# A hybrid trunk on Trainium2: ring units over low and high parts of a tile, first pair picked in turned form, last gated product first

## The chip, the cores and the metric

The kernel runs on one core of a Trainium2 chip. Its engines are TensorE (PE, with its weight loads shown as PEld), VectorE (DVE), ScalarE (ACT), GpSimd (POOL) and SyncE (SP), which here only issues DMAs. The metric is the device time of one execution in microseconds; of several runs the median counts.

## What is computed

One layer of a decoder trunk over 512 tokens of width 1024, everything in float32: RMSNorm, four token mixers with gates, an output projection, and a mixture of experts. The change touches what comes from the output projection on:

```python
x = x + h @ w_out                          # (512, 1024), h: gated sum of the mixers
xn = rms_norm(x, ffn_norm_g)
# router: the best of 4 groups, then the best 2 of its 8 experts, with weights
for e in range(32):                        # 32 experts, hidden width 256
    hid = silu(t @ w_expert_gate[e]) * (t @ w_expert_up[e])
    out = out + combine[:, e:e + 1] * (hid @ w_expert_down[e])
return rms_norm(x + out, final_norm_g)
```

Every expert has three matrices of 1 MB: 96 MB of weights for the experts alone.

## The kernel before

Tokens are handled in four tiles of 128 (NT = 4); width 1024 is KC = 8 chunks of 128. All engines run programs of their own, written out by hand, and meet at semaphores only.

**Output products** (from L1990 on, products at L1999). Eight groups n = 0 to 7: the first four make columns 0 to 511 of the four tiles, the second four columns 512 to 1023. Each is 8 chunks of three products (high and low parts of h and w_out: hh, hl, woh, wol). Between the chunks stand the router's transposes (L1948), its logits (L1958) and the rank counts (rank_products, L1969) of the tile before. DVE adds the residual (L1108) and picks experts (`route`), ACT squares.

**First pair.** Experts run in pairs, with up to 64 tokens of each. For the first pair DVE makes 0/1 columns `chosen`, and TensorE picks the tokens' rows of x2 by products with them (choose_rows, L2005): `chosen` are the weights, x2 the moving operand of 512 columns, and the result lies in banks 0 and 1 with tokens on partitions. ACT (L1014) and DVE (L1430) copy the two banks to `xg[:, 0]`; TensorE turns them chunk by chunk (x_transposes, L2112), and DVE multiplies them with the norm's gain into xT (x_out, L1451). For all later turns GpSimd gathers rows from x2_dram by indirect DMA (L717) into xg. `first_table` makes the table of slots (L2022, L1977) after the last choose_rows.

**Expert turns** (expert_pass, L2110 to L2190 for TensorE). 17 turns: 15 whole pairs, and two further ones for the fullest expert and its partner. A turn is gate products and up products (L2146), hid = up times silu(gate) on DVE (L1087, a helper's line), two transposes (L2155), and down products (L2172). Results of a turn are scattered to y_dram by GpSimd (L724); those of the last two turns (KEPT) stay on chip as yeh and yel and are added by products with `pick` (kept_products, L2077).

**Ring of weights.** SP loads 1 MB units (load_unit_no, L518), in the order gate, gate, up, up, down, down of every pair, into NU = 21 slots (raw_slots), unit w into slot w mod 21. A unit above 20 waits until the products that read its slot are done (wait_reuse). The first 21 are loaded as room comes free: 10 before the output products, units 10 to 13 after their first half, 14 and 15 (ring_p0 over hl of tiles 0 and 1, ring_p1 over hh of tiles 0 and 1) after tile 1 of the second half, 16 to 20 (ring_e0, ring_e1 over parts of woh and wol, ring_q over hh of tiles 2 and 3) after all output products. In the same queue stand the stores of x2 (L567), one for each tile.

**End.** SP waits for the scatters, loads the gathered results y of tile 1 (EARLY_ROWS), the last two down units, then the results of tiles 0, 2, 3 and the final gain gfin, spread over all partitions. DVE adds weighted results (gather_results), in turn LAST for tile 1 before it makes hid. TensorE sums in PSUM (TOTALS) for tiles 0 and 1; DVE adds PSUM sums for tiles 2 and 3 (added, L1658). ACT squares with a sum, and takes the root (final_norm, L1059, L1061); DVE scales with the reciprocal and gfin (scaled, L1650, L1087), in the order 0, 2, 1, 3, and SP stores (L608). The code after `If(most > SLOT)` handles experts with more tokens and is not run on these inputs.

## Time and profile before

| | |
|---|---|
| three runs | 720.05, 722.11, 722.59 us; median 722.11 us |
| profiled execution | 720.5 us, its span 718.4 us |
| TensorE clock granted, mean | 0.995 of full speed |
| busy | PE 97%, PEld 72%, DVE 52%, ACT 36%, POOL 11% |
| DMA | 163.52 MB, mean 228 GB/s |
| chain that ended last | PE 90%, DMA 4%, DVE 3% |

The profile is one execution. A busy TensorE is not one at its peak, as products are pipelined. The page's slices of the span (40 equal ones, 18 us each, busy share in tenths) show when an engine works; the windows view gives the same for stretches that one names, with the share of time in which the 16 DMA engines were busy and what they moved. "[0.82 <-DVE chosen L1391]" behind an instruction says that its engine was idle for 0.82 us before it, and what ended that.

### The profile page before, as it was taken

The page shows a single profiled execution, that of the slowest core. Times are in us where ns is not written, and L with a number is a line of the kernel's source. Part 1 is how long each engine was busy: PE and PEld are TensorE (multiplying, and loading weights), DVE is VectorE, ACT ScalarE, POOL GpSimd, SP SyncE. Part 2 cuts the span into 40 slices and gives each one's busy share as a digit, 9 for nine tenths or more (in the row PEclk, how much of TensorE's full clock was granted, in tenths as well). Part 3 has the DMA queues.
Part 4 walks back from the last instruction along what each step waited for, and adds up shares of the span by engine and source line. Part 5 has one row for each costly group of instructions (what it writes and reads, how often), then busy time and mean ns, then how long its engine had stood idle before and what let it go on. Part 6 is the DMA issues. An engine that isn't in the chain of part 4 may idle for free.

```text
span 718.4 us, 10092 instructions
## 1 busy us (share of the span) xinstructions
PE 698.4 (97%) x3967; PEld 514.5 (72%) x3967; DVE 371.8 (52%) x727; ACT 256.4 (36%) x426; POOL 80.1 (11%) x116
## 2 busy tenths in 40 slices
PE   7999999999999999999999999999999999999894
PEld 6888987877877777788888888665555556555442
DVE  6378996357676778755536303751514121212227
ACT  7332134467676776644225212121101111111113
POOL 2001922000010101000003000011211212121000
PEclk9999999999999999999999999999999999999998
DMA  7523244220212222295214598699999999999993
GB/s 240 174 66 111 65 121 147 74 73 16 68 66 73 74 74 74 82 381 181 91 56 183 219 416 303 266 368 365 408 418 419 401 421 421 418 420 417 419 375 141
DMA packets 60208, 163.52 MB, mean 228 GB/s; under 512 B 7846, under 2 KB 39667, under 8 KB 47868
## 3 DMA queue, kind: packets, MB, share of 16 engines
q1 hardware_dynamic: 54668, 150.71, 55.3%
q0 software_dynamic: 5488, 12.11, 4.5%
q8 instruction: 33, 0.54, 0.3%
q14 instruction: 19, 0.16, 0.1%
HBM read 154.64 MB, written 15.99 MB: 238 GB/s over the span
## 4 chain that ended last, share of the span: by engine, by line
PE 90%; DMA 4%; DVE 3%; ACT 1%; issue 1%; SPq 0%; POOLq 0%; DVEq 0%; ACTq 0%
PE psum L1719 31%; PE psum L2146 15%; PE psum L1820 12%; PE psum L2172 8%; PE psum L1999 6%; PE psum L1832 3%; PE psum L2112 2%; DMA ring_e<-y_dram 2%; DVE ring_e L1087 2%; PE psum L1845 1%; PE psum L1875 1%; DMA y_dram<-ye,slots 1%; PE psum L2155 1%; PE psum L1958 1%; PE psum L1910 1%; PE psum L1898 1%
## 5 line engine op out<-in xcount | busy, mean ns | idle before, releaser
L1719 PE MATMUL psum<-xh,wh 128*128 128x512 f32 x256 | 99.9, 390 | 0.8 <-DVE xl L1087 0.8
L1719 PE MATMUL psum<-xh,wl 128*128 128x512 f32 x256 | 99.6, 389 | 0.0
L1719 PE MATMUL psum<-xl,wh 128*128 128x512 f32 x256 | 99.6, 389 | 0.0
L1090 DVE TENSOR_TENSOR wl<-raw,wh 128x1280 fp32r<-128x1280 f32 (+4 forms) x37 | 71.8, 1945 | 24.7 <-ACT wh L780 9.0
L1087 DVE SCALAR_TENSOR_TENSOR hid<-psum,rslot,act_g 128x256 f32<-128x256 f32 x17 | 8.2, 483 | 93.4 <-PE psum L2146 92.8
L1719 PEld LDWEIGHTS psum<-xh,wh 128*128 128x128 f32 x256 | 48.1, 188 | 11.1 <-DVE xl L1087 1.0
L1719 PEld LDWEIGHTS psum<-xh,wl 128*128 128x128 f32 x256 | 48.0, 188 | 9.9
L1719 PEld LDWEIGHTS psum<-xl,wh 128*128 128x128 f32 x256 | 48.1, 188 | 9.8
L1820 PE MATMUL psum<-xh,wh 128*128 128x512 f32 x128 | 51.7, 404 | 0.0
L1820 PE MATMUL psum<-xh,wl 128*128 128x512 f32 x128 | 50.1, 391 | 0.0
L1820 PE MATMUL psum<-xl,wh 128*128 128x512 f32 x128 | 49.9, 390 | 0.0
L1087 DVE SCALAR_TENSOR_TENSOR sg<-cu,ch,sg 128x512 f32<-128x512 f32 x60 | 48.7, 882 | 0.0
L2146 PE MATMUL psum<-ring_w,xT 128*64 128x256 f32 x256 | 38.8, 383 | 0.0
L1036 ACT ACTIVATE act_g<-psum,rslot 128x256 f32<-128x256 f32 x17 | 8.1, 474 | 78.5 <-PE psum L2146 72.7
L1038 ACT ACTIVATE hidT<-psum 128x256 f32<-128x256 f32 x17 | 6.5, 384 | 78.1 <-PE psum L2155 78.1
L1640 DVE COPY ye<-psum 128x512 f32<-128x512 f32 x15 | 10.4, 691 | 44.6 <-PE psum L2172 44.6
L724 POOL DMA_INDIRECT y_dram<-ye,slots x15 | 15.1, 1009 | 158.0 <-DVE ye L1640 114.5
L1311 DVE TENSOR_TENSOR gp<-gs,psum 128x512 f32<-128x512 f32 x16 | 11.0, 687 | 36.9 <-PE psum L1719 36.1
L2146 PEld LDWEIGHTS psum<-ring_w,xT 128*64 128x64 f32 x256 | 22.3, 136 | 10.5 <-issue 3.4
L958 ACT ACTIVATE gs<-psum,bg 128x512 f32<-128x512 f32 x16 | 10.9, 687 | 50.3 <-PE psum L1719 50.3
L1820 PEld LDWEIGHTS psum<-xh,wl 128*128 128x128 f32 x128 | 24.0, 188 | 5.2
L1820 PEld LDWEIGHTS psum<-xl,wh 128*128 128x128 f32 x128 | 24.1, 188 | 4.8 <-issue 0.2
(386 smaller groups left out, 1539.6 us busy)
## 6 DMA issues: line engine op xcount, KB each, us to landing
raw<-in_w_gate SPq DMA_DIRECT2D x16, 1024.0 KB, 6.4
raw<-in_w_in SPq DMA_DIRECT2D x9, 1024.0 KB, 5.5
ring_w<-in_w_expert_gate SPq DMA_DIRECT2D x8, 1024.0 KB, 19.8
ring_w<-in_w_expert_up SPq DMA_DIRECT2D x8, 1024.0 KB, 22.4
ring_h<-in_w_expert_down SPq DMA_DIRECT2D x8, 1024.0 KB, 16.5
ring_h<-in_w_expert_gate SPq DMA_DIRECT2D x6, 1024.0 KB, 18.2
ring_e<-in_w_expert_down SPq DMA_DIRECT2D x6, 1024.0 KB, 23.1
ring_e<-in_w_expert_gate SPq DMA_DIRECT2D x6, 1024.0 KB, 21.4
```

Source lines behind the costliest of these rows:

```text
L724: pool.indirect_dma_start(out=y_dram[:, :], out_offset=bass.IndirectOffsetOnAxis(ap=slots[n, p], axis=0), in_=ye[n, :], in_offset=None, bo ...
L958: act.activation(gs[:, m, :], gate_bank(cg, m)[:, :], ACT.Sigmoid, bias=bg[:, d:d + 1]).then_inc(S["gate_mul"], 1)
L1087: return dve.scalar_tensor_tensor(out=out_, in0=a, scalar=s, in1=b, op0=o0, op1=o1)
L1090: return dve.tensor_tensor(dst, src, hi.bitcast(F32), ALU.subtract)
L1311: dve.tensor_tensor(gp[:, m, :], gs[:, m, :], branch_bank(cg, m)[:, :], ALU.mult).then_inc(S["gate_free"], 1)
L1719: last = nc.tensor.matmul(dst, a, b, start=start and n == 0, stop=stop and n == len(seq) - 1)
L1820: last = nc.tensor.matmul(bank[6 + n % 2][:, :], a[:, c, f], b[:, c, :], start=c == 0 and q == 0, stop=c == KC - 1 and q == 2)
L1832: last = nc.tensor.matmul(bank[4 + n % 2][:, :], a[:, j, f], b[g][:, j, :], start=j == 0 and q == 0, stop=j == BJ - 1 and q == 2)
L1999: last = nc.tensor.matmul(bank[t][:, :], x_[:, t, c, :], w_[:, b, c, :], start=c == 0 and m == 0, stop=c == KC - 1 and m == 2)
L2112: last = nc.tensor.transpose(bank[b][:, (k % 4) * P:(k % 4 + 1) * P], xg[:, s, :].rearrange("p (n c) -> p c n", c=KC)[:, k, :], ident[:, :])
L2146: last = nc.tensor.matmul(dst[half, 0:FE], xT[:, k, half], w[h][:, k, :], start=k == 0, stop=k == KC - 1)
L2172: last = nc.tensor.matmul(bank[5 + b][half, :], hidT[:, m, half], w_d[h][:, m, b * T:(b + 1) * T], start=m == 0, stop=m == FE // P - 1)
```

## The change

1. **Ring slots over the parts of one tile.** ring_p0, ring_p1, xg and ring_q become one buffer ring_p of shape [2, NT, D]: [0, t] lies over hl of tile t, [1, t] over hh of tile t. Slots 14, 15 and 16 are its tiles 0, 1 and 2, each of two runs of 1024 values per partition; xg (and yel) is tile 3. Slots 17 to 20 are ring_e0 and ring_e1, first their first units, which lie over chunks 0 to 3 of woh and wol. All slots, and the source of all loads, are written as [2, 1024] per partition.
2. **Release.** Unit 14 + t is loaded after output tile t of the second half, ahead of the tile's store of x2; 17 and 18 after chunk 3 of the last tile (out_ps is raised there too), 19 and 20 after its end.
3. **First pair.** choose_rows takes the chunks of x2 as weights and `chosen` as moving operand, 8 products of 128 columns for a tile, so that the result lies turned in banks 0 and 1. The copies to xg and the first x_transposes go. GpSimd clears both halves of xg rather than one.
4. **Last gated product first.** In turn LAST gather_results for tile 1 follows hid.
5. **Tile 0's norm.** DVE takes the reciprocal of tile 0 only; ACT scales tile 0 (ACT.Copy with a scale), GpSimd multiplies with gfin, SP stores it first.

The rest of the diff counts semaphores anew.

```diff
-        ring_p0 = sb(moe, "ring_p0", [1, UNIT_E])
         kept_l = region()
-        yel = sb(kept_l, "yel", [KEPT, D], F32R)
+        yel = sb(kept_l, "yel", [KEPT, NT, D], F32R)[:, :, NT - 1, :]
         kept_l.close()
-        xg = sb(moe, "xg", [2, D])
-        ring_p1 = sb(moe, "ring_p1", [1, UNIT_E])
-        ring_q = sb(moe, "ring_q", [1, UNIT_E])
+        ring_p = sb(moe, "ring_p", [2, NT, D])
+        xg = ring_p[:, :, NT - 1, :]
...
-        raw_slots = ([r[:, n, :] for r in (ring_z, ring_x) for n in range(2)] + [ring_y[:, n, :] for n in range(2)]
-                     + [ring_w[:, n, :] for n in range(4)] + [ring_h0[:, 0, :], ring_h0[:, 1, :], ring_h1[:, 0, :], ring_h2[:, 0, :]]
-                     + [ring_p0[:, 0, :], ring_p1[:, 0, :]] + [r[:, n, :] for r in (ring_e0, ring_e1) for n in range(2)]
-                     + [ring_q[:, 0, :]])
-        AFTER_GATES, AFTER_HALF, AFTER_PAIR, AFTER_OUT = 10, 14, 16, 21
+        raw_slots = [r[:, n, :].rearrange("p (j n) -> p j n", j=2) for r, n in (
+            [(r, n) for r in (ring_z, ring_x, ring_y) for n in range(2)] + [(ring_w, n) for n in range(4)]
+            + [(ring_h0, 0), (ring_h0, 1), (ring_h1, 0), (ring_h2, 0)])]
+        raw_slots += [ring_p[:, :, t, :] for t in range(NT - 1)]
+        raw_slots += [r[:, n, :].rearrange("p (j n) -> p j n", j=2) for n in range(2) for r in (ring_e0, ring_e1)]
+        AFTER_GATES, AFTER_HALF, AFTER_TILES, AFTER_PART, AFTER_OUT = 10, 14, 17, 19, 21
...
-        yt = [raw_slots[n].rearrange("p (j n) -> p j n", j=2) for n in (16, 17, 18, 19)]
-        gfin = raw_slots[20][:, 0:D]
+        yt = raw_slots[16:20]
+        gfin = raw_slots[20][:, 0, :]
...
-                sp_e.dma_start(raw_slots[slot], weights(*units_of(c)[w], found)).then_inc(ring_full[slot], 16)
+                sp_e.dma_start(raw_slots[slot], weights(*units_of(c)[w], found).rearrange("p (j n) -> p j n", j=2)).then_inc(ring_full[slot], 16)
...
             for t in range(NT):
+                if t == NT - 1:
+                    sp_e.wait_ge(S["out_ps"], 2 * NT)
+                    for w in range(AFTER_TILES, AFTER_PART):
+                        load_unit_no(w)
+                else:
+                    sp_e.wait_ge(S["out_ps"], NT + t + 1)
+                    load_unit_no(AFTER_HALF + t)
                 sp_e.wait_ge(S["x2_ready"], NT + t + 1)
                 sp_e.dma_start(x2_dram[t * P:(t + 1) * P, :], x2[:, t, :]).then_inc(S["x2_out"], 16)
-                if t == 1:
-                    sp_e.wait_ge(S["out_ps"], NT + 2)
-                    for w in range(AFTER_HALF, AFTER_PAIR):
-                        load_unit_no(w)
-            sp_e.wait_ge(S["out_ps"], 2 * NT)
-            for w in range(AFTER_PAIR, AFTER_OUT):
+            sp_e.wait_ge(S["out_ps"], 2 * NT + 1)
+            for w in range(AFTER_PART, AFTER_OUT):
...
+                    if base == 0 and t == 0:
+                        continue
+                    sp_e.wait_ge(S["fin_last"], base + n + (1 if base else 0))
                     sp_e.dma_start(out_v[t], yt[t][:, 1, :]).then_inc(S["out_done"], 16)
...
+            sp_e.wait_ge(S["norm_step"], 3)
+            sp_e.dma_start(out_v[0], yt[0][:, 1, :]).then_inc(S["out_done"], 16)
             store_results(0)
...
-            pool.wait_ge(S["out_ps"], 2 * NT)
-            st.link(pool.memset(xg[:, 1, :], 0.0))
+            pool.wait_ge(S["out_ps"], 2 * NT + 1)
+            st.link(pool.memset(xg[:, :, :], 0.0))
...
+            pool.wait_ge(S["tab_in"], 48)
+            pool.wait_ge(S["norm_step"], 2)
+            pool.tensor_tensor(halves(yt[0][:, 1, :]), halves(yt[0][:, 1, :]), halves(gfin), ALU.mult).then_inc(S["norm_step"], 1)
...
-            act.wait_ge(S["routed_ps"], NT + 1)
-            act.activation(xg[:, 0, 0:T], bank[0][:, :], ACT.Copy).then_inc(S["moved_a"], 1)
...
                 if t < ADDED:
                     act.wait_ge(S["c_ps"], SUMMED.index(t) + 1)
                     final_norm(n, t, TOTALS[t], 3 * NT)
+                    if t == 0:
+                        act.wait_ge(S["comb"], 3)
+                        act.activation(halves(yt[0][:, 1, :]), TOTALS[0], ACT.Copy, scale=stat[:, 2, 0:1]).then_inc(S["norm_step"], 1)
...
-                dve.wait_ge(S["out_ps"], b * NT + t + 1)
+                dve.wait_ge(S["out_ps"], 2 * NT + 1 if b and t == NT - 1 else b * NT + t + 1)
...
-            dve.wait_ge(S["routed_ps"], NT + 2)
-            dve.tensor_copy(xg[:, 0, T:2 * T], bank[1][:, :]).then_inc(S["hot_ready"], 1)
...
-                        gather_results(1, EARLY_ROWS)
                     dve.wait_ge(S["silu"], E + 1)
                     dve.wait_ge(S["gu_done"], E + 1)
                     stt(hid[:, :], bank[3][:, 0:FE], rslot[:, column(c, i)], act_g[:, :], ALU.mult, ALU.mult).then_inc(S["hid_r"], 1)
+                    if isinstance(c, int) and i == LAST:
+                        gather_results(1, EARLY_ROWS)
...
+            dve.wait_ge(S["root"], NT + 2 + NORMED.index(0))
+            dve.reciprocal(stat[:, 2, 0:1], stat[:, 1, 0:1]).then_inc(S["comb"], 1)
             added(2)
-            first_scaled(0)
             added(3)
             first_scaled(2)
             first_scaled(1)
             first_scaled(3)
...
+                    if n == 2 * NT - 1 and c == KC // 2 - 1:
+                        last.then_inc(S["out_ps"], 1)
                 last.then_inc(S["out_ps"], 1)
             def choose_rows(t, b):

                 pe.wait_ge(S["hot_ready"], CHOSEN[t])
-                return nc.tensor.matmul(bank[b][:, :], chosen[:, t, :], x2[:, t, b * T:(b + 1) * T], start=t == 0, stop=t == NT - 1)
+                for k in range(4 * b, 4 * b + 4):
+                    last = nc.tensor.matmul(bank[b][:, (k % 4) * P:(k % 4 + 1) * P], x2[:, t, :].rearrange("p (n c) -> p c n", c=KC)[:, k, :],
+                                            chosen[:, t, :], start=t == 0 and k % 4 == 0, stop=t == NT - 1, skip_group_check=True)
+                return last
...
-                choose_rows(NT - 1, b).then_inc(S["routed_ps"], 1)
+                choose_rows(NT - 1, b).then_inc(S["xt_ps"], 1)
...
-                if isinstance(c, int) and i == 0:
-                    pe.wait_ge(S["moved_a"], 2 * NT + 1)
-                    pe.wait_ge(S["hot_ready"], ALL_HITS + 1)
-                elif b == 0:
+                if b == 0:
...
-                for b in range(2):
-                    x_transposes(c, 0, first % 2, b)
+                if not isinstance(c, int):
+                    for b in range(2):
+                        x_transposes(c, 0, first % 2, b)
...
-                        w = [loaded(h, kind).rearrange("p (c f) -> p c f", f=FE) for h in halves]
+                        w = [loaded(h, kind).rearrange("p j (c f) -> p j c f", f=FE) for h in halves]
...
-                                last = nc.tensor.matmul(dst[half, 0:FE], xT[:, k, half], w[h][:, k, :], start=k == 0, stop=k == KC - 1)
+                                last = nc.tensor.matmul(dst[half, 0:FE], xT[:, k, half], w[h][:, k // 4, k % 4, :], start=k == 0, stop=k == KC - 1)
...
-                    w_d = [loaded(h, 2).rearrange("p (m n) -> p m n", m=FE // P) for h in halves]
+                    w_d = [loaded(h, 2) for h in halves]
```

## Rows read from the trace of the kernel before

**Rows 1.** The page: busy share of the DMA engines in tenths, 40 slices of the span.
```profile
DMA  7523244220212222295214598699999999999993
```
**Rows 2.** Windows: stretch, its us, busy per engine, PEclk, DMA share, GB/s.
```profile
456.00:458.00 2.00, 2.00 (x12) 1.69 (x12) 1.54 (x8) 0.00 (x0) 0.00 (x0) 1.00 0.01 4
...
474.00:476.00 2.00, 2.00 (x22) 1.60 (x20) 1.70 (x13) 1.53 (x3) 1.63 (x2) 1.00 0.86 303
...
660.00:680.00 20.00, 17.13 (x118) 10.13 (x116) 4.42 (x7) 2.19 (x5) 1.01 (x1) 1.00 1.02 420
```
**Rows 3.** DMA view: us to landing of loads issued at 462.7, 475.4, 642.1, 677.5.
```profile
ring_q<-in_w_expert_up SPq DMA_DIRECT2D x1, 1024.0 KB, 14.4
...
ring_z<-in_w_expert_up SPq DMA_DIRECT2D x1, 1024.0 KB, 7.0
...
ring_x<-in_w_expert_up SPq DMA_DIRECT2D x1, 1024.0 KB, 29.4
...
ring_h<-in_w_expert_down SPq DMA_DIRECT2D x1, 1024.0 KB, 17.5
```
**Rows 4.** Timeline of PE, turns 15 and 16: start, us, what, idle before.
```profile
671.65 3.67 PE L2146 MATMUL psum<-ring_x,xT 128*64 128x256 f32 x32 [1.34 <-DMA ring_x<-in_w_expert_up]
...
695.50 3.65 PE L2172 MATMUL psum<-ring_h,hidT 128*64 128x512 f32 x16
```
**Rows 5.** Timeline, the end: VectorE and ScalarE.
```profile
692.68 0.48 DVE L1087 SCALAR_TENSOR_TENSOR hid<-psum,rslot,act_g 128x256 f32<-128x256 f32 x1
...
700.59 1.27 DVE L1087 SCALAR_TENSOR_TENSOR ring_e<-ring_e,cw,x 128x1024 f32<-128x1024 f32 x1
...
712.62 1.28 DVE L1087 SCALAR_TENSOR_TENSOR ring_e<-ring_e,stat,ring_q 128x1024 f32<-128x1024 f32 x1
...
709.14 1.02 ACT L1059 ACTIVATE ring_e<-psum 128x1024 f32<-128x1024 f32 x1 [0.49 <-PE psum L2077]
```
**Rows 6.** Timeline of SP's issues around the output products' second half.
```profile
439.15 7.23 SPq L567 DMA_DIRECT2D x_dram<-x  x2
...
460.39 1.25 SPq L518 DMA_DIRECT2D ring_e<-in_w_expert_down  x2
...
475.40 0.33 SPq L518 DMA_DIRECT2D ring_z<-in_w_expert_up  x1
```
**Rows 7.** Timeline of PE from the choosing products to the first gate product.
```profile
462.38 3.68 PE L2005 MATMUL psum<-x,chosen 128*128 128x512 f32 x8
...
467.20 1.98 PE L2005 MATMUL psum<-x,chosen 128*128 128x512 f32 x4 [0.82 <-DVE chosen L1391]
...
470.06 1.12 PE L2112 MATMUL psum<-ident,xg 128*128 128x128 f32 x8
471.69 0.65 PE L2146 MATMUL psum<-ring_z,xT 128*64 128x256 f32 x4 [0.51 <-DVE xT L1451]
```
**Rows 8.** Timeline of VectorE in the same stretch.
```profile
465.82 0.24 DVE L1087 SCALAR_TENSOR_TENSOR rmask<-re,rs,ro 128x32 bf16<-128x32 f32 x1
...
468.42 0.48 DVE L1380 TENSOR_SCALAR hot<-slot_no,rank 128x128 fp32r<-128x128 f32 x2
```
**Rows 9.** Timeline of PEld: eight weight loads of transposes and of router logits.
```profile
470.03 0.95 PEld L2112 LDWEIGHTS psum<-ident,xg 128*128 128x128 f32 x8
...
461.46 0.97 PEld L1958 LDWEIGHTS psum<-wr,xt 128*128 128x128 f32 x8
```
**Rows 10.** DMA view of 691 to 695, mostly packets of 4 KB.
```profile
DMA packets 386, 1.64 MB, mean 410 GB/s; under 512 B 42, under 2 KB 42, under 8 KB 330
```
**Rows 11.** Timeline: a GpSimd addition; one beside VectorE; VectorE alone.
```profile
85.47 3.42 POOL L665 TENSOR_TENSOR axb<-axb,gs 128x512 f32<-128x512 f32 x1
...
173.13 0.74 POOL L682 TENSOR_TENSOR run<-run,sp 128x256 f32<-128x256 f32 x1
...
173.29 1.00 DVE L1090 TENSOR_TENSOR spl<-sp,sph 128x384 fp32r<-128x384 f32 x1
...
178.36 0.56 DVE L1090 TENSOR_TENSOR run_l<-run,run_h 128x384 fp32r<-128x384 f32 x1 [0.63 <-ACT run_h L949]
```

More of the change, by code:

```diff
@@ L308, in hybrid_trunk @@
             "hi_part xg_ps xg_neg xg_min xg_ln xg_max xg_exp xb_ps xg_free gate_ps br_ps gate_free gate_mul h_add h_hi h_split out_ps x2_ready "
-            "wo_in wo_hi wo_split g_in tab_in x2_out xt2_ps moved_a lg_ps sq2_sum wr_ready slots_in flag_ready lg_act lg_in m_ready routed_ps "
+            "wo_in wo_hi wo_split g_in tab_in x2_out xt2_ps moved_a lg_ps norm_step wr_ready slots_in flag_ready lg_act lg_in m_ready routed_ps "
             "hot_ready slot_ps idx_ready over_ready rs_in rs_ps rs_ready rank_ready turns gf0 gf1 w_ps pick_ready y_hi y_lo y_zero xt_ps xe g_done gu_done silu hid_r "
@@ L623, in _ @@
                 load_results(range(NT))
-                store_results(NT)
+                store_results(NT - 1)
                 sp_e.wait_ge(S["out_done"], 2 * (16 * NT))
@@ L1009, in _ @@
                 token_squares(n)
-            act.wait_ge(S["sq2_sum"], 1)
+            act.wait_ge(S["norm_step"], 1)
             act.activation(stat[:, 1, :], stat[:, 0, :], ACT.Sqrt, bias=eps[:, 0:1], scale=1.0 / D).then_inc(S["root"], 1)
-            act.wait_ge(S["routed_ps"], NT + 1)
-            act.activation(xg[:, 0, 0:T], bank[0][:, :], ACT.Copy).then_inc(S["moved_a"], 1)
             act.wait_ge(S["lg_in"], 1)
@@ L1067, in _ @@
                     final_norm(n, t, TOTALS[t], 3 * NT)
+                    if t == 0:
+                        act.wait_ge(S["comb"], 3)
+                        act.activation(halves(yt[0][:, 1, :]), TOTALS[0], ACT.Copy, scale=stat[:, 2, 0:1]).then_inc(S["norm_step"], 1)
                 else:
-                    act.wait_ge(S["comb"], 2 + t - ADDED + 1)
+                    act.wait_ge(S["comb"], 3 + t - ADDED + 1)
                     final_norm(n, t, halves(yt[t][:, 0, :]), 3 * NT)
@@ L1077, in _ @@
                 for n, t in enumerate(NORMED):
-                    act.wait_ge(S["fin_last"], NT + n)
+                    act.wait_ge(S["fin_last"], NT - 1 + n)
                     final_norm(n, t, TOTALS[t], 4 * NT)
@@ L1422, in _ @@
             dve.wait_ge(S["sq_done"], 3 * NT)
-            dve.reduce_sum(stat[:, 0, :], sq_part[:, :, :], AX.X).then_inc(S["sq2_sum"], 1)
+            dve.reduce_sum(stat[:, 0, :], sq_part[:, :, :], AX.X).then_inc(S["norm_step"], 1)
             for part in range(2):
@@ L1671, in _ @@
             with dve.If(most[0] > SLOT):
-                dve.wait_ge(S["comb"], 2 + NT - ADDED)
+                dve.wait_ge(S["comb"], 3 + NT - ADDED)
                 for t in range(NT):
@@ L2064, in table_products @@
                 if i == SPILL and k == 0:
-                    pe.wait_ge(S["hot_ready"], ALL_HITS + 2)
+                    pe.wait_ge(S["hot_ready"], ALL_HITS + 1)
                     slot_products()
@@ L2188, in _ @@
                 with pe.Fori(1, PASSES) as c:
-                    pe.wait_ge(S["hot_ready"], c + (ALL_HITS + 2))
+                    pe.wait_ge(S["hot_ready"], c + (ALL_HITS + 1))
                     slot_products()
```

1 line of the change is left out of this document (removed).

## The prediction

> **What bounds the kernel now.** I read the windows view first. From 500 us on the 16 DMA engines are busy all the time [rows 1], in 660 to 680 at 420 GB/s while TensorE has 2.9 us idle [rows 2]. The landings say which of the two decides. A unit issued at 475.4 lands 7.0 us later, the second up unit of turn 15, issued at 642.1, after 29.4 us, at 671.5 [rows 3]: the queue falls further behind in every turn, and the 21 units loaded ahead pay for it until they are used up. That happens in turn 15: TensorE starts the up products at 671.65 after a wait of 1.34 us for that load [rows 4]. The last down unit was issued at 677.5 and landed 17.5 us later, at 695.0 [rows 3], and the last down products started at 695.5 [rows 4]. So the end of the expert stage is set by the DMA queue, not by TensorE. Its length is fixed; what counts is when it gets its work, and that is when ring units come free. After 700 the chain is VectorE: four gathered rows, four additions and four scalings nearly without a gap, from 700.59 to the last scaling at 712.62 [rows 5], then a store.
>
> The queue has one large hole: a share of 0.01 in 456 to 458 [rows 2], because the last five ring units are issued only when the last tile of output products ends (460.4 and after) [rows 6]. Unit 20 of them took 14.4 us from 462.7, so landed at 477.1 [rows 3], just after turn 0 released the first slots and two more loads went out at 475.4 [rows 6].
>
> **The change part by part.**
>
> *First pair picked in turned form.* Now: choose_rows for the last tile (467.20), the slot table, then eight transposes (470.06) of rows that ACT and DVE first had to copy to xg, then DVE's xT, then the gate products at 471.69 [rows 7]. After: no copies, no transposes; DVE's xT can start when DVE is free of its last hot columns, 468.42 + 0.48 = 468.9 [rows 8], so its first half is ready at 469.65 and TensorE goes from the table (ends 470.1) straight into the gate products. Gain 471.69 - 470.1 = 1.6 us, and DVE's tables and the first gathers follow as much earlier. The price is in choose_rows: one tile was 2 products of 512 columns, 4 instructions of about 0.43 us, since eight of them took 3.68 with the end of the last [rows 7]: 1.7 us. It becomes 8 products of 128 columns, 16 instructions, each with its own weights. The trace shows no such product. Nearest are eight transposes of 128 columns, whose weight loads follow each other at (0.95 - 0.19) / 7 = 0.109 us, and eight instructions of ordinary fp32 products with 36 columns at (0.97 - 0.19) / 7 = 0.111 [rows 9]. 16 x 0.11 = 1.8 us: the same as before. I take 0.11, the value of both rows. Tiles 1 and 2 then end at about 462.4 + 3.6 = 466.0, which just meets rmask at 465.82 + 0.24 [rows 8]; beyond 0.11 each instruction is on the path.
>
> *Ring units released tile by tile.* Units 14, 15, 16 go out as tiles 0, 1, 2 of the second half end (about 438.5, 445.5, 452.5: the store of tile 0 starts at 439.15, the loads behind the store of tile 3 at 460.39, so a tile takes about 7 us [rows 6]), 17 and 18 in the middle of the last tile (about 455.5), 19 and 20 at 460.4. In SP's queue the stores of x2 stand between them: each is still behind its own tile, and the last one, at 460.0, is now behind 5 us of loads, landing near 465; only the first gather needs it, which comes behind DVE's slot columns, after 470. The ring is then full at about 468 rather than 477. But this alone only moves the hole: there are 21 slots either way, and the 22nd load must wait for turn 0. What is gained is that the queue is empty when turn 0 releases slots, where before it still had about 1.5 us of unit 20 to do. Against that, the releases of turn 0 come more slowly than an empty queue serves them (three pairs, one behind each kind of product, the first at 475.4 [rows 6]), so part is lost again: before, the share was already down to 0.86 in 474 to 476 [rows 2]. I work with 0.7 of the 1.5, bounds 0 and 1.5.
>
> The shift of all releases by 1.6 us moves the end of the DMA queue by the full 1.6, since the work after it is the same. TensorE shifts by 1.6 too and has waits for loads in turn 15 to give up, 1.34 us in one of them alone [rows 4], so it follows the DMA.
>
> *Rows of a unit cut in two.* Slots 14, 15, 16 now consist of two runs of 4 KB per partition instead of one of 8 KB. The stretch of mostly 8 KB packets moved 420 GB/s [rows 2], one of mostly 4 KB packets 410 [rows 10]: 2.4% less, 0.06 us of the 2.5 us that 1 MB takes at 420 GB/s. Nine such units go out after turn 0 begins: 0.5 us. Sum for the DMA end: 1.6 + 0.7 - 0.5 = 1.8 us earlier (bounds 1.1 to 2.6).
>
> *Last gated product first.* DVE now adds the early gathered rows (two of 1.28) before the last hid, which therefore follows them without a gap at 692.68 [rows 5], though its up products ended near 691.6. Moved behind it, hid comes 1.0 us earlier. But the down products behind it need the last down unit, which lands at 695.0, 0.5 us before they start now [rows 3, 4]. Only 0.45 us can be had. The gathered rows themselves are needed by nothing before 700: free.
>
> *Tile 0's norm off VectorE.* One scaling of 1.28 and its reciprocal of 0.15 leave the DVE chain, 0.15 comes back: 1.28 less [rows 5]. ACT gets a copy of 1.03 us, in an idle stretch, GpSimd a product of 128 x 1024. What is late next: ACT squares tile 1 at 709.14, right behind TensorE [rows 5], so its root is there at about 710.6 (1.02 and the two small steps behind it, 0.5), DVE's scaling of tile 1 fills 710.6 to 712.05 (0.15 + 1.28), and the one of tile 3 can start at 712.2 instead of 712.62. So 0.4 us are left of the 1.28. GpSimd took 0.74 us for 256 columns, in another place 3.42 for 512 [rows 11], so 3.0 to 6.8 us for 1024. Started near 705 it ends by 708 to 712; the last store waits on SP behind it only from 711.3 on. Also DVE is slowed beside it: a difference of 384 columns took 1.00 us when GpSimd ran an addition of 0.74, and 0.56 alone [rows 11]. One scaling (two operands from SBUF) lies beside the GpSimd product; with the same ratio it costs 0.4 to 1.0 us, of which about 0.5 is free. I take 0.45 lost, bounds 0 and 1.0. So the rows show interference; the Trainium skill (GPSIMD Engine Reference, Specifications) says that GpSimd's SBUF interfaces are shared with VectorE and contend with instructions that have two SBUF inputs, which agrees with the 0.56 against 1.00.
>
> *The rest:* clearing both xg slots is 1.9 instead of 0.95 us of GpSimd at 459.3, with 12 us until the first gather; the view of weights as [2, 4, 256] has the same addresses in all slots but three; both cost nothing on the path.
>
> **Sum.** 1.8 + 0.45 + 0.4 - 0.45 = 2.2 us. The profiled execution took 720.5 us (span 718.4 and 2.1 around it) and would take 718.3. The median of the three runs is 722.1, 1.6 above the profiled one, with 2.5 us between the lowest and the highest. The same 2.2 off the median, with a little for the uncertain term of GpSimd, is 719.8.
>
> **Rivals.**
> 1. *Every unit is cut in two.* The change rewrites all loads as [2, 1024] per partition. If the transfer is not put together again where the two halves touch, all units after turn 0, some 75, cost 0.06 more: 4.5 us instead of 0.5 in a queue that sets the end. The result is 2.2 - 4.0, so 1.8 us slower: 723.9. Without any cut unit the gain is 2.7; the point from which the change loses is 2.7 / 0.06 = 45 cut units. For it: the text of the loads. Against it: the two halves are contiguous on both sides in 18 of 21 slots. Packet counts under 8 KB tell it at once. The Trainium skill (DMA: Bandwidth & Descriptors, Why a DMA increments its semaphore by 16 and not by 1) says that one descriptor moves one contiguous run of the last dimension; taken by the letter that is this rival. No row of before shows which it is. Chance 0.15.
> 2. *The turned products are slower than 0.11 us an instruction,* say 0.17, as when a weight load is not hidden behind the product before it. Then 16 take 2.7 us: 0.5 late at tile 0, 1.7 at tiles 1 and 2, 0.9 at tile 3, some of it shared with DVE's waits; the 1.6 us gain becomes a loss near 1.0. Result 2.2 - 2.6: 722.5. Against it: both nearest rows have 0.11 with a new weight load for every instruction. Chance 0.10.
> 3. *The early ring units are worth more,* the full 1.5 us, and GpSimd disturbs nothing: gain 3.5, 718.6. With a measured median on the kind side this is beyond 0.5%. Chance 0.15.
> 4. Forecast, 719.8, own range 718.5 to 721.2: chance 0.60.
>
> **Chances.** 0.5% is 3.6 us, about what a measurement of this kernel can tell from no change. Case 4 reaches that only by the spread of medians (one in six, 0.10), case 3 in about half: faster 0.18. Slower by more than 3.6 us needs rival 1 with a larger price for a cut unit (with 3% it would be 5.6 us) and an unkind median: 0.06. The rest, 0.76, is no change that can be told. Range 717.4 to 723.6: it leaves out the far ends of cases 1 and 3.
>
> **What would show it.** First gate products at 470.1 instead of 471.7, with no transposes before; 48 more instructions of choose_rows at 0.11 us; a DMA share near 1 in 446 to 452 and a new hole between 468 and 474; last down unit landing at about 693.2; last hid some 2.8 us earlier; last store at about 711.7 instead of 713.9. Packets under 8 KB up by some 3000 (12 units) if the halves are joined, by over 20000 if not. Wrong would be: an unchanged landing of the last down unit with the earlier turn 0, or a GpSimd product that ends after 711.

## The result: 8 us slower

| | before | after |
|---|---|---|
| runs | 4: 720.05 to 722.59 us, median 721.3 | 4: 727.46 to 730.62 us, median 729.74 |
| ratio | | 1.0106, 95% interval 1.0073 to 1.014 |
| profiled execution | 720.5 us, span 718.4 | 730.62 us, span 728.4 |

The prediction was 719.8, range 717.4 to 723.6: wrong in sign and outside its range. The profiled executions lie 10.0 us apart in span, so this is the difference that the rows have to explain.

The page of the kernel after: the clock granted to TensorE, the DMA share, and packets.

```profile
PEclk9999999999999999999999999979999999999998
DMA  7523234221212121493305789839999999999993
DMA packets 61745, 163.53 MB, mean 225 GB/s; under 512 B 7846, under 2 KB 39667, under 8 KB 50940
```

The DMA row has a new hole (the 3 in the 27th slice, 473 to 492 us; before a 9 [rows 1]) and PEclk has its only 7 in the same slice. The timeline of TensorE in that stretch, after (start, us, what, xcount, idle before it):

```profile
461.38 2.07 PE L2018 MATMUL psum<-chosen,x 128*128 128x128 f32 x8
...
464.25 7.86 PE L2018 MATMUL psum<-chosen,x 128*128 128x128 f32 x32
...
472.90 4.18 PE L2018 MATMUL psum<-chosen,x 128*128 128x128 f32 x16 [0.70 <-DVE chosen L1401]
...
477.03 1.87 PE L1987 MATMUL psum<-rv,hot 128*128 128x32 f32 x8
478.83 6.47 PE L2159 MATMUL psum<-ring_z,xT 128*64 128x256 f32 x32
```

L2018 is choose_rows. Its 32 instructions for tiles 1 and 2 take 7.86 us, the 16 for tile 3 take 4.18; by [rows 7] it was 3.68 and 1.98. The gate products start at 478.83, 7.1 us later than in [rows 7], and take 6.47 us. At full clock the same 32 instructions take 3.67, as in the kernels below. The weight loads of the picking set the pace:

```profile
464.23 7.70 PEld L2018 LDWEIGHTS psum<-chosen,x 128*128 128x128 f32 x32
472.90 3.89 PEld L2018 LDWEIGHTS psum<-chosen,x 128*128 128x128 f32 x16 [0.80 <-DVE chosen L1401]
```

They follow each other at 0.24 us, where the weight loads of [rows 9] had 0.11. The windows show the clock (column behind the five engines) and the DMA share:

```profile
472.00:474.00 2.00, 1.30 (x10) 1.20 (x8) 1.50 (x12) 0.00 (x0) 0.00 (x0) 1.00 0.00 0
474.00:476.00 2.00, 2.00 (x10) 2.00 (x10) 1.27 (x5) 0.00 (x0) 0.00 (x0) 0.57 0.00 0
...
480.00:482.00 2.00, 2.00 (x12) 1.08 (x10) 1.67 (x10) 1.03 (x3) 1.27 (x2) 0.50 0.00 0
```

By these windows the granted clock falls to 0.50, the 1.2 GHz level, near 474.3, and it is back near 484.5 (0.87 in 484 to 486). Before the fall lie 15 us in which TensorE had mostly these slow products and one pause of 0.70. The queue of loads is empty all that time; before, the share in 474 to 476 was 0.86 [rows 2]. Unit 21 is issued at 485.35, not at 475.40 [rows 6].

**Where the 10 us are.** From the first picking product (459.16, before 459.04) to the first up product (485.13, before 475.17) after needs 25.97 us and before 16.13: 9.84 more. With the 0.12 us of the later start, up products and unit 21 are 10.0 late. The last down unit is issued and lands so:

```profile
ring_h<-in_w_expert_down SPq DMA_DIRECT2D x1, 1024.0 KB, 18.7
```

Issued at 687.04, landed at 705.74, 10.7 later than in [rows 3]. From there to the start of the last scaling it is 16.92 us, before 17.62: the tail has gained 0.70. The queue loses another 0.7 behind unit 21, as much as the tail gains, so 10.0 + 0.7 - 0.7 = 10.0. The loss lies in the 26 us around the picking.

### The profile page after: what moved, and what is told of

It reads as the page before. It is cut to its first block, busy times and chain, and to the rows that moved or that the text cites. A ratio compares the mean times of both kernels' runs of the same rounds, so it can differ in the third digit from the quotient of the medians.

```text
span 728.4 us, 10171 instructions
## 1 busy us (share of the span) xinstructions
PE 709.7 (97%) x4007; PEld 528.5 (73%) x4007; DVE 370.8 (51%) x725; ACT 256.9 (35%) x426; POOL 83.2 (11%) x117
## 4 chain that ended last, share of the span: by engine, by line
PE 91%; DMA 4%; DVE 2%; ACT 1%; issue 1%; SPq 0%; DVEq 0%; ACTq 0%; POOLq 0%
PE psum L1729 30%; PE psum L2159 15%; PE psum L1830 12%; PE psum L2185 8%; PE psum L2009 6%; PE psum L1842 3%; DMA ring_h<-in_w_expert_down 3%; PE psum L2018 2%; PE psum L2124 2%; PE psum L1855 1%; PE psum L1885 1%; DVE ring_e L1097 1%; DMA y_dram<-ye,slots 1%; PE psum L2168 1%; PE psum L1968 1%; PE psum L1920 1%
```

## The experiments

Theory S: a weight load of an fp32 product whose values lie 32 bytes apart takes twice as long; that is the loss, and the fall of the clock follows from it. Rival N: narrow products (128 columns moved) cost 0.24 at any step. Rival R: the early ring units take part in it. Of each kernel two stretches of its profiled execution are compared, (a) from the first picking product to the first gate product and (b) from there to the first up product, 3.50 us at full clock; beside them stands the time of its runs. A kernel with a single run has no interval.

| kernel | (a) us | (b) us | median us, runs | ratio to before, interval |
|---|---|---|---|---|
| before | 12.65 | 3.48 | 721.3 | |
| after | 19.67 | 6.30 | 729.74, 4 | 1.0106, 1.0073 to 1.014 |
| e1_old_pick | 12.66 | 3.48 | 721.77, 10 | 1.0005, 0.9987 to 1.0022 |
| e2_turned_alone | 18.98 | 3.50 | 729.11, 5 | 1.0103, 1.0085 to 1.0121 |
| e3_contiguous | 11.18 | 3.50 | 719.87, 10 | 0.9969, 0.9953 to 0.9985 |
| e4_strides | 15.95 | 6.36 | 726.4, 1 | |
| e5_columns | 18.17 | 3.51 | 726.87, 1 | |
| e6_twice | 17.91 | 3.50 | 726.63, 6 | 1.0071, 1.0046 to 1.0095 |
| e7_last_tile | 14.12 | 5.36 | 723.51, 1 | |
| e8_ordered | 11.17 | 3.50 | 720.7, 12 | 0.9985, 0.9969 to 1.0001 |
| e9_ordered_alone | 11.17 | 3.50 | 722.67, 10 | 1.0007, 0.9987 to 1.0028 |
| e10_ordered_again | 11.16 | 3.50 | 720.23, 12 | 0.9974, 0.9959 to 0.9989 |

**e1_old_pick: the change without its picking.**

```diff
-                for k in range(4 * b, 4 * b + 4):
-                    last = nc.tensor.matmul(bank[b][:, (k % 4) * P:(k % 4 + 1) * P], x2[:, t, :].rearrange("p (n c) -> p c n", c=KC)[:, k, :],
-                                            chosen[:, t, :], start=t == 0 and k % 4 == 0, stop=t == NT - 1, skip_group_check=True)
+                return nc.tensor.matmul(bank[b][:, :], chosen[:, t, :], x2[:, t, b * T:(b + 1) * T], start=t == 0, stop=t == NT - 1)
```

The copies to xg and the first transposes are back as well.

> The changed kernel with the old way of picking the first pair (products of 512 columns with `chosen` as weights, two copies, eight transposes); ring units, order of hid, tile 0's norm as changed. Theory S (the loss is the turned picking: its products take 0.24 us each instead of 0.11 because their weights are read with a step of 32 bytes, and the granted clock falls to half behind them) and rival N (it is the turned picking, but because narrow products with new weights for each cost that much whatever the step) expect the same here: first gate product at 471.7 as before, no fall of the clock, and a time within 1.5 us of before, rather below it (0 to 1 us less: about 0.8 from the end, against 0.5 for units cut in two). Rival R (the early ring loads take part in the loss) expects 2 us or more above before.

Measured: 721.77 us, no difference to before that can be told. Ring, tail and norm together are not the loss, and no gain that the times can show either. In the profiled execution the gate products start at 471.91, and the clock is 1.00 up to there.

**e2_turned_alone: the picking alone, on the kernel before.**

```diff
-                return nc.tensor.matmul(bank[b][:, :], chosen[:, t, :], x2[:, t, b * T:(b + 1) * T], start=t == 0, stop=t == NT - 1)
+                for k in range(4 * b, 4 * b + 4):
+                    last = nc.tensor.matmul(bank[b][:, (k % 4) * P:(k % 4 + 1) * P], x2[:, t, :].rearrange("p (n c) -> p c n", c=KC)[:, k, :],
```

> The kernel before with the turned picking alone. S and N: 8 to 10.5 us slower than before, first gate product near 478.8, granted clock at half for some 5 to 10 us. Rival R: less than 7 us slower, the rest of the loss being in the ring loads.

Measured: 729.11 us, ratio 1.0103 where the whole change has 1.0106. The 1.03% are 7.4 us, a little less than the 8 that S and N expected and a little more than the 7 of rival R. What lets R fall is that the picking alone costs as much as the whole change, and that e1_old_pick is not 2 us above before. The profiled execution, 726.02 us, was the quickest of five: its clock was at 0.50 only from about 473.9 to 477.3 (the two windows below hold this stretch, so their means are 0.89 and 0.77) and was back when the gate products ran, as (b) shows. The other four, with a mean clock of 0.986 to 0.992 against its 0.995, took 729.06 to 730.23. They have no profile, but it looks as if the time that the clock stays low differs from execution to execution, and is worth some 3 to 4 us.

```profile
470.00:475.00 5.00, 4.30 (x22) 4.18 (x22) 2.08 (x15) 0.00 (x0) 0.00 (x0) 0.89 1.02 431
475.00:480.00 5.00, 5.00 (x39) 4.33 (x40) 2.91 (x10) 0.00 (x0) 0.30 (x1) 0.77 0.05 20
```

**e3_contiguous: weights without a step.** Chunk k takes 128 neighbouring columns, so the first pair gets its inputs in a wrong order; all instructions and waits stay.

```diff
-x2[:, t, :].rearrange("p (n c) -> p c n", c=KC)[:, k, :],
+x2[:, t, k * P:(k + 1) * P],
```

> The changed kernel, but choose_rows takes 128 neighbouring columns of x2 as weights instead of every eighth: the first pair's experts get their inputs in the wrong order, all instructions and sizes are the same. S: 0.11 us an instruction, first gate product at 470.1 to 470.5, clock not falling, and 719 to 720.5 us (the time that was predicted for the change, or a little more). N: 0.24 us an instruction, 729 us, as the changed kernel. If the products become fast and the clock falls nevertheless, it is not their length that lets it fall: then about 724.

Measured: 719.87 us, faster than before. The timeline of TensorE:

```profile
464.19 3.82 PE L2018 MATMUL psum<-chosen,x 128*128 128x128 f32 x32
...
469.03 2.05 PE L2018 MATMUL psum<-chosen,x 128*128 128x128 f32 x16 [0.82 <-DVE chosen L1401]
...
471.02 1.04 PE L1987 MATMUL psum<-rv,hot 128*128 128x32 f32 x8
472.00 3.67 PE L2159 MATMUL psum<-ring_z,xT 128*64 128x256 f32 x32
```

3.82 where after had 7.86, 2.05 where it had 4.18, and the clock stays at 1.00. In this execution and in e5_columns the first picking product comes 1.7 and 1.6 us later than in the others (460.82 and 460.70), because the clock had been at 0.50 for 3.4 us near 144 us (0.57 in the mean of 144 to 148); so one compares stretches, not points in time. For the slow products S is shown and N falls: nothing but the address step was changed. That the fall of the clock follows from them is what e6_twice and e7_last_tile test.

**e4_strides: which step.** Tile t takes weights 2^t values apart: 4, 8, 16 and 32 bytes (the first pair's inputs are in a wrong order).

```diff
-x2[:, t, :].rearrange("p (n c) -> p c n", c=KC)[:, k, :],
+x2[:, t, :].rearrange("p (a n s) -> p a s n", s=2 ** t, n=P)[:, k // 2 ** t, k % 2 ** t, :],
```

> The changed kernel with another step between the weights in each tile's choose_rows: 4 bytes in tile 0, 8 in tile 1, 16 in tile 2, 32 in tile 3 (the first pair's inputs come in the wrong order, sizes are the same). S: 0.11 us an instruction in tile 0, 0.24 in tile 3, and the steps between tell from where it costs. N: 0.24 in all four.

Measured from start to start of the instructions: 0.111 us at 4 bytes, 0.118 at 8, 0.233 at 16, 0.239 at 32. It is a jump between 8 and 16 bytes, not a growth with the step. Tiles 1 and 2 together and tile 3:

```profile
462.55 5.86 PE L2020 MATMUL psum<-chosen,x 128*128 128x128 f32 x32
...
469.21 4.18 PE L2020 MATMUL psum<-chosen,x 128*128 128x128 f32 x16 [0.70 <-DVE chosen L1401]
```

Half of the products are slow here, and the clock falls all the same (0.50 in 472 to 480), gate products 6.53 us.

**e5_columns: does what moves matter?** Tile 0: step 32 bytes, 128 columns; tile 1: step 32, 64 columns; tile 2: contiguous, 64; tile 3: contiguous, 128. Part of the first pair's sums is left out.

```diff
+                    spread, cols = ((True, P), (True, SLOT), (False, SLOT), (False, P))[t]
...
-                                            chosen[:, t, :], start=t == 0 and k % 4 == 0, stop=t == NT - 1, skip_group_check=True)
+                                            chosen[:, t, 0:cols], start=t == 0 and k % 4 == 0, stop=t == NT - 1, skip_group_check=True)
```

> The kernel after, where the picking products of tile 0 take weights with 32 bytes from one to the next and move 128 columns, those of tile 1 the same weights but move only 64 columns, tile 2 contiguous weights and 64 columns, tile 3 contiguous weights and 128 columns (so the first pair's rows are not the right ones). Theory that the step between the weights alone sets the pace: instructions follow each other at 0.24 us in tiles 0 and 1 and at 0.11 us in tiles 2 and 3, whatever moves. Rival, that weight load and products add up: tile 1 near 0.21, tile 2 near 0.08. Time by the theory: tiles 0 and 1 late as in the kernel after, tiles 2 and 3 as with contiguous weights, so 719.9 + 16 x 0.13 = about 722 without a fall of the clock (some of tile 0's delay lies beside the wait for the mask), 3 more with one.

Measured: 0.238 us in tile 0 and 0.240 in tile 1, so the number of moved columns has no part in it. Tiles 2 and 3, 0.213, looked like a miss, until one reads the clock of the stretch:

```profile
466.00:470.00 4.00, 4.00 (x18) 4.00 (x19) 3.51 (x18) 1.38 (x2) 0.00 (x0) 0.72 1.02 424
470.00:472.00 2.00, 2.00 (x12) 2.00 (x11) 0.05 (x1) 0.00 (x0) 0.00 (x0) 0.50 0.87 369
```

At 0.50 a contiguous load takes 0.213, nearly twice 0.111. The strided loads do not get slower by it: in after, tile 3's loads took 0.238 before and after the clock went from 1.00 to 0.50. The clock fell here before TensorE had any pause: it is 0.95 in 466 to 468, and the only pause, of 0.70, ends at 474.06. The time, 726.87, is one run, 1.9 above the 725 expected with a fall of the clock; 1.6 of it are the late start of the picking, from the fall near 144 us.

**e6_twice: the delay without the slow loads.** Contiguous weights, each product made twice into the same sum (the first pair's rows are doubled and in a wrong order).

```diff
                 for k in range(4 * b, 4 * b + 4):
+                    for again in range(2):
```

> The kernel after with contiguous weights and every picking product made twice, into the same sums (so the first pair's rows are not the right ones): 128 products instead of 64 at 0.11 us an instruction take nearly the time of 64 at 0.24, but TensorE is fed at full pace. If the clock falls after the turned products because they feed TensorE slowly, it stays at 1.00 here: the gate products start near 477.5 to 478 and take 3.5 us, about 5.5 to 6 late, 726. If it is the delay itself, or the pause in front of the last tile, that draws the clock down, it falls here too: gate products of 6.3 us, 729 to 730.

Measured: 726.63 us. The stretch to the gate products is 6.73 us longer than in e3_contiguous, the clock is 1.00 in all of it, and the median is 6.76 longer. So the delay is passed on to the end, in full as far as the runs can tell: the intervals leave some 2 us on either side, and in the two profiles the last down unit lands 5.9 later, counted from the first picking product.

```profile
464.05 7.39 PE L2019 MATMUL psum<-chosen,x 128*128 128x128 f32 x64
...
472.24 3.84 PE L2019 MATMUL psum<-chosen,x 128*128 128x128 f32 x32 [0.70 <-DVE chosen L1401]
...
476.99 3.67 PE L2160 MATMUL psum<-ring_z,xT 128*64 128x256 f32 x32
...
459.00:476.00 17.00, 16.30 (x153) 16.12 (x152) 9.12 (x47) 2.79 (x5) 1.80 (x1) 1.00 0.67 281
```

There is the same pause of 0.70 and nearly the same delay as in after, but no fall of the clock. So neither the pause nor the delay draws it down here; what differs is that TensorE takes in weights and columns at the full pace. This is one profile; the mean clock of this kernel's six runs is 0.991 to 0.997, that of after's four 0.988 to 0.994. In the profiles after needs 4.56 us more than this kernel up to the first up product. Of these, 3.63 are the half clock (2.80 in the gate products, 0.83 in the table's products at L1987, 1.87 against 1.04), the rest is in the picking, which is still a little longer in after. The medians lie 3.1 apart.

**e7_last_tile: only tile 3 with the step.**

```diff
+                    weights_of = x2[:, t, :].rearrange("p (n c) -> p c n", c=KC)[:, k, :] if t == NT - 1 else x2[:, t, k * P:(k + 1) * P]
```

The first pair's inputs of tiles 0 to 2 are in a wrong order.

> The kernel after with contiguous weights in tiles 0 to 2 and weights with a step of 32 bytes in tile 3 only (so the first pair's rows are not the right ones). 16 instructions at 0.24 instead of 0.11 us: 2.1 us late against the kernel with contiguous weights everywhere, 719.9 + 2.1 = 722.0, if the clock stays at 1.00 because the slow stretch is only 4 us long. Rival: the pause in front of tile 3 and the 4 us behind it are enough for the clock to fall: gate products over 5 us instead of 3.5, 724 to 725.

```profile
467.42 4.18 PE L2019 MATMUL psum<-chosen,x 128*128 128x128 f32 x16 [0.82 <-DVE chosen L1401]
...
471.54 1.87 PE L1987 MATMUL psum<-rv,hot 128*128 128x32 f32 x8
473.34 5.52 PE L2160 MATMUL psum<-ring_z,xT 128*64 128x256 f32 x32
```

My expectation was wrong, its rival right: the clock fell (0.57 in 470 to 472, then 0.50), behind a pause of 0.82 and 16 slow products. The same pause with 16 products at 0.111 left it at 1.00 (e3_contiguous). This rests on one run; its time, 723.51, is a little under the rival's 724 to 725.

**e8_ordered: contiguous weights by a copy.** ScalarE copies each finished tile of x2 into chunk order, over the parts of tiles 0 and 1 in ring_p; units 14 and 15 are loaded after the last picking product.

```diff
+        ordered = [ring_p[:, t % 2, t // 2, :] for t in range(NT)]
...
+                act.activation(ordered[t].rearrange("p (c n) -> p c n", c=KC), x2[:, t, :].rearrange("p (n c) -> p c n", c=KC),
+                               ACT.Copy).then_inc(S["h_hi"], 1)
...
+                    pe.wait_ge(S["h_hi"], KC + t + 1)
...
+            sp_e.wait_ge(S["xt_ps"], 2)
+            for w in range(AFTER_HALF, AFTER_HALF + 2):
+                load_unit_no(w)
```

> The kernel after, computing the right thing, with contiguous weights: ScalarE copies each tile of x2, when it is complete, into an order in which every chunk is contiguous (four copies of 128x1024, about 1.2 us each where ScalarE has its time), and the picking products read the copies. These lie over the parts of tiles 0 and 1 in ring_p, so units 14 and 15 are loaded only after the last picking product, near 470. Theory: instructions at 0.11 us, clock 1.00, gate products 1.6 us earlier than before; the two units are loaded in the hole of the DMA queue that the change opened, of which up to 0.7 us of gain may be lost: 720.0 to 720.6, so faster than both kernels, by 1.2 to 1.9 us against before. Rival: ScalarE's read with a step is slow as well (over 2 us a copy) or tile 3's copy ends after its columns: then the gate products are late and it is no better than before, 722 or more.

```profile
470.29 3.67 PE L2174 MATMUL psum<-ring_z,xT 128*64 128x256 f32 x32
...
462.71 2.05 ACT L1023 ACTIVATE ring_p<-x 128x1024 f32<-128x1024 f32 x1
...
470.00:480.00 10.00, 10.00 (x84) 6.49 (x83) 5.03 (x31) 1.70 (x3) 2.10 (x2) 1.00 0.92 354
```

The gate products start at 470.29; the prediction had said 470.1. ScalarE's copy took 2.05 to 2.16 us, not 1.2, so the rival was right on the copy but not on what it does: ScalarE had the time, tile 3's ends at 464.8, its columns come at 467.3. The hole of the queue is filled, share 0.92 where after has 0.02. The time is 720.7 us with an interval that just touches no change, so I ran it again.

**e10_ordered_again: the same kernel, more runs.**

> The kernel e8_ordered again, unchanged, for a narrower interval on whether it beats the kernel before. From the rows: 1.4 us on the gate products, 0.7 in the tail, so 719.5 to 720.5 and a ratio of 0.997 to 0.998; if the ring's late units take part of it back, a ratio of 0.999 to 1.000.

Measured: 720.23 us, ratio 0.9974, interval 0.9959 to 0.9989. In these runs it beats before by 0.26% (0.1 to 0.4), in those of e8_ordered by 0.15% (0 to 0.3); an estimate from both intervals is 0.2% (0.1 to 0.3). It beats after by over 1%.

**e9_ordered_alone: the ordered copies on the kernel before, without ring and tail.**

The diff of e8_ordered and e2_turned_alone together, with

```diff
+        ordered = [r[:, 0, h * D:(h + 1) * D] for h in range(2) for r in (ring_p0, ring_p1)]
```

> The kernel before with the turned picking from copies in order (as e8_ordered), and nothing else of the change: old ring, old tail. Units 14 and 15 are loaded after the last picking product here as well, but the five units 16 to 20 go out only at 460.4, as before, so the queue has seven units (17.5 us) to do from 462 on. TensorE's part is that of e8_ordered: instructions at 0.111 us, gate products near 470.3. Theory that the early ring units are worth something only as room for what is loaded late: here the queue is still busy until near 482 when turn 0 has released its first slots at 474, so unit 21 lands 2 to 3 us later than in e8_ordered (485 against 482.4), the first gather is late for turn 1, and with the old tail (0.7) the time is 2.5 to 4 us above e8_ordered, 723 to 725. Rival, that the queue has slack enough in turns 0 to 2 to catch up: only the tail is missing, 0.7 above e8_ordered, 721.4.

Measured: 722.67 us, 2.4 above e10_ordered_again, and its profiled execution, in which the clock fell twice, is 4.3 longer in span. Unit 21, issued at 473.96, lands at 485.77; in e8_ordered, issued at 474.00, at 482.45. The gathered rows of turn 1 come late:

```profile
481.10 1.10 PE L2118 MATMUL psum<-ident,xg 128*128 128x128 f32 x4 [0.87 <-DMA xg<-x_dram,toks]
...
480.00:484.00 4.00, 3.13 (x16) 2.27 (x14) 1.72 (x4) 0.86 (x2) 0.00 (x0) 0.66 1.01 410
...
492.00:500.00 8.00, 8.00 (x45) 5.08 (x47) 0.00 (x0) 0.00 (x0) 0.00 (x0) 0.68 1.03 418
```

In the profiles, then, the early ring units do have a worth where something else is loaded late. Of the 2.4 us the old tail is 0.7; how much of the rest is the queue and how much the clock this pair doesn't tell apart. The time is 2.0 above e8_ordered, under the 2.5 to 4 that I expected, and the rival (0.7 above) can't be ruled out by times: the ratio lies 0.33% over that of e10_ordered_again and 0.22% over that of e8_ordered, each with about 0.25% on either side. Against before there is no difference that can be told, so the ordered copies alone gain nothing.

## Why the prediction was wrong, step by step

**The bound: right.** That the end is set by the DMA queue, and that it moves with the release of slots in turn 0, holds: e6_twice passed 6.73 us of delay on as 6.76, known to some 2 us.

**First pair in turned form: here it failed.** The step is "16 x 0.11 = 1.8 us: the same as before. I take 0.11, the value of both rows." An instruction took 0.238, so a tile 3.8 us.
The bill against e3_contiguous, which has the length that I had priced, by stretches of the two timelines: tile 0 and what stands between, 1.72 us; tiles 1 and 2, 3.81; tile 3 and the table, 2.96, of which 0.83 is the table at half clock; gate products at half clock, 2.80. Sum 11.29 up to the first up product. Against before, 1.45 are gained back, as the copies and transposes are gone: 9.84. The predicted gain of that part, 1.6, was thus right but for the length of the products: e3_contiguous and e8_ordered show 12.65 - 11.17 = 1.5.

**The clock: not in the prediction at all.** No step asked what a stretch of slow products does to it. It made 3.6 of the 11.3 us in the profiled execution. No rival of the prediction had it either.

**Ring units released tile by tile: right in kind, worth nothing.** The ring was full at 471.9, not at 468, since the queue still needed 11 us for the units issued at 461. In e1_old_pick, with the releases of turn 0 at the times of before, the second unit of turn 0 takes 8.71 us to land, before 9.37: 0.66 gained, where I had 0.7. But the fourth, issued 0.2 later than before, takes 7.32 against 7.38. By then the gain is gone: in turns 0 and 1 the queue waits for releases, so an earlier start is given back at the next one. The window of the hole was the reason that I gave myself and then weighed too lightly.

**Units cut in two: right.** 3072 more packets under 8 KB are 12 units of 256, so only the three slots in ring_p are cut and rival 1 fell. The Trainium skill's rule (DMA: Bandwidth & Descriptors, Why a DMA increments its semaphore by 16 and not by 1), taken by the letter, would have cut all units; the trace doesn't agree. From the issue of unit 21 to the landing of the last down unit it is 219.4 to 220.5 us in the eight profiles with cut units and no later fall of the clock (mean 219.9), and 219.6 and 218.9 in the two without (before, e2_turned_alone). That is 0.7 more in the mean, near my 0.5, but the eight alone scatter over 1.1; it isn't settled by these.

**Last gated product first: right.** Timeline of the end, after:

```profile
702.40 0.48 DVE L1097 SCALAR_TENSOR_TENSOR hid<-psum,rslot,act_g 128x256 f32<-128x256 f32 x1 [8.10 <-PE psum L2159]
...
717.69 2.38 POOL L764 TENSOR_TENSOR ring_p<-ring_p,ring_e 128x1024 f32<-128x1024 f32 x1 [39.25 <-ACT ring_p L1077]
...
719.11 0.16 DVE L1659 RECIPROCAL stat<-stat 128x1 f32<-128x1 f32 x1 [0.35 <-ACT stat L1068]
719.31 1.85 DVE L1097 SCALAR_TENSOR_TENSOR ring_e<-ring_e,stat 128x1024 f32<-128x1024 f32 x1
721.08 0.15 DVE L1659 RECIPROCAL stat<-stat 128x1 f32<-128x1 f32 x1
...
722.66 1.28 DVE L1097 SCALAR_TENSOR_TENSOR ring_e<-ring_e,stat 128x1024 f32<-128x1024 f32 x1
```

hid starts 3.3 us and is out 2.9 us before the last down unit lands at 705.74. In e3_contiguous the last down products start 0.14 us behind that landing, before 0.50 [rows 3, 4]: 0.36 gained, predicted 0.45.

**Tile 0's norm: right in mechanism, wrong in size.** From the start of the last down products to the last scaling it is 17.12 us before and 16.78 in e3_contiguous: 0.34 gained, where the sum had 0.4 - 0.45, a loss of 0.05. GpSimd's product took 2.38 us, below my bounds of 3.0 to 6.8, worked out from operations elsewhere in the kernel [rows 11]. It does slow VectorE: the scaling of tile 2, beside it for its first 0.76 us, took 1.85, not 1.28. But these 0.57 us lie in a wait for tile 1's root, the very next thing that I had named: that root is ready at 720.95 and its reciprocal starts at 721.08, the scaling of tile 2 ends at 721.16, so nearly nothing is lost.

**The sum: right in size, in part by luck.** With the picking at the length that I had priced the forecast was 2.2 us below before; e3_contiguous is 0.31% below, 2.2 us, interval 1.1 to 3.4. But the parts, as the profiles show them, are others: 1.5 from the picking, nothing from the ring where I had 0.7, 0.7 lost (not settled) to cut units where I had 0.5, and 0.70 from the tail where I had 0.4. They add up to 1.5. The tail's 0.70 is the same in every profile with the new tail (landing of the last down unit to the issue of the last store, 18.23 to 18.24 us; before, e2_turned_alone and e9_ordered_alone 18.93 to 18.94). My 1.8 us for the DMA end, bounds 1.1 to 2.6, was too high: counted from the first picking product, the last down unit lands 0.6 us earlier than before in e3_contiguous and 1.05 in e8_ordered. In e1_old_pick, without the gain of the picking, the 0.70 of the tail and the 0.7 of the queue cancel, which fits its time. None of this turns the sign; the term that did was the picking's, wrong by a factor of two in a count of 64.

**What stays open.** Why a load slows down at 16 bytes, and only in ordinary fp32 products and not in transposes. What lets the clock fall: it did so during the picking in all five profiles with strided weights, and in none of the seven others between 400 us and the gate products, but with one profile a kernel that is a coincidence of stretches and no mechanism. It falls elsewhere without them, too: near 144 us in e3_contiguous and e5_columns, from 481 and from 495 in e9_ordered_alone, and in e1_old_pick in 494 to 500, in a stretch where before kept 1.00:

```profile
494.00:500.00 6.00, 6.00 (x30) 3.85 (x30) 0.00 (x0) 0.00 (x0) 0.00 (x0) 0.54 1.00 413
```

## What to carry to other kernels

Price an operation by a row that has the same operand in the same role with the same step between its values, and where there is none, let the range reach to twice the nearest row, above all when the term is a large count times a small duration. To turn fp32 data by using it as weights, have it contiguous (or at most 8 bytes apart, as measured here) first; a copy on an engine with time to spare paid for itself here, though only together with the ring and the tail (0.2% under before) and not alone (e9_ordered_alone). A delay in the stage that feeds the saturated DMA queue was passed on to the end, while an earlier start of the queue was given back where it next waited for releases.

## What the runs showed of the hardware

- Weight loads of 128 columns in ordinary fp32 products follow each other at 0.111 us with 4 bytes from value to value, 0.118 with 8, 0.233 with 16, 0.239 with 32 (e4_strides); with 64 moved columns instead of 128 and 32 bytes it is still 0.240 (e5_columns). Those of transposes at 32 bytes: 0.11 [rows 9].
- At a granted clock of 0.50 contiguous products took 0.213 instead of 0.111 (e5_columns), the strided ones 0.238 as before (after, tile 3): the slow loads don't follow the clock.
- In 400 to 712 us the clock's falls add up to 3.4 to 5.1 us of lost time (half of the time at 0.50) in four of the five profiles with strided weights and to 1.7 in e2_turned_alone. Up to the gate products there are none in the five with contiguous ones only; behind them there are 5.1 in e9_ordered_alone, and 3.4 in e1_old_pick.
- The spread of the kernel before goes with such falls as well: of 61 of its runs the 17 with a mean clock of 0.996 and more took 720.2 us on average (719.3 to 721.3), the 12 with 0.990 and less 723.6 (721.6 to 725.4).
- ScalarE's copy of 128x1024 from values 32 bytes apart took 2.05 to 2.16 us (e8_ordered), and its copy of the same size from PSUM, without a step, 1.12 (tile 0's norm, after).
- A VectorE scaling of 128x1024 with two operands from SBUF took 1.85 us when a GpSimd product of the same size ran beside it for its first 0.76 us, and 1.28 alone (after).
